# Feed-forward activations turned by VectorE in 32x32 blocks and a trip through a DRAM scratch, in place of TensorE transposes

## The chip, the cores and the metric

The kernel runs on one core of one Trainium2 chip. The metric is the device time of one execution in microseconds (us), lower is better. The kernel before was timed in 3 runs.

## The reference, cut to what matters

The program is a net of four layers on one sequence of 256 rows and 1024 features, in float32. Two layers mix retention, chunked attention and differential attention, two mix an mLSTM with windowed attention. Each layer has one or two gated feed-forward parts, six in all, and only these are touched:

```
ffn = (silu(x @ w_gate) * (x @ w_up)) @ w_down      # x: 256 x 1024
```

The hidden width is 2816 in the two feed-forwards of the first kind of layer, and 2752 in the four of the second kind. TensorE contracts over the partitions of its operands. So the product `silu(...) * (...)`, which comes out with the 256 rows on partitions (two tiles of 128), must stand with its features on partitions before it can be multiplied by `w_down`. Turning it is what the change does in another way.

## The kernel before

**Precision.** All large products are made of float32 values split in two parts: a high part, rounded to the type of TensorE's fast mode, and the rest, the low part. A product takes three matmuls: high by high, high by low, low by high. For weights, ScalarE makes the high part (`wh`, step "hi", line 1270) and VectorE the low part (`wl`, step "lo", line 1499).

**Units.** The weights stream from DRAM in 776 units of mostly 128 x 1024 elements (512 KB), issued by SP (line 1095) into a ring `raw` of 13 slots. The load of unit u+13 waits until TensorE has done unit u. `wh` has 10 slots, so step "hi" of unit u+10 waits for TensorE to be done with unit u. One unit of the feed-forward is two k-tiles of 128 by 512 columns, for two row tiles: 12 matmuls of 512 columns (lines 1957, 1961, 1962).

**The order of work.** A planner writes one list of steps, and each engine walks through the whole list and executes its own part of every step, in that order. `place_splits` puts the "hi" and "lo" steps between the others as far ahead of their unit as the slots allow. Around the end of each large product stand `tail` and `open`: they run the units of a group first for row tile 0 and then for row tile 1, so that the normalization of one tile lies beside the matmuls of the other. In `open` the first 6 to 8 units of a feed-forward go by twice like this.

**One feed-forward** (`plan_ffn`). Its gate and up weights come in 11 chunks of 256 hidden features: four units, which fill two PSUM banks (one for each row tile) with 256 gate and 256 up columns. The pairs of banks alternate. After the units of chunk c the list has:

- `swiglu` (c): ScalarE makes silu into `ffn_s` (line 1465), VectorE multiplies by the up columns into `ffn_a` (line 1887 where the row scale of the norm is applied too, line 1889 otherwise). Both buffers have two slots, by the parity of c.
- `split_act` (c-1): TensorE turns four 128x128 pieces of `ffn_a` by transposes with an identity into a PSUM bank `TB` (line 2018), ScalarE copies it to the high part `act_h` (line 1291), VectorE subtracts to get the low part `act_l` (line 1518; lines 1506 to 1510 for the last chunk of width 192).

The last chunk's `split_act` stands behind the second unit of the down product (`BEHIND = 1`). Then come 22 units of the down product, which read `act_h` and `act_l` as the stationary operand. The transposes that the change takes away are in TensorE's branch

```
elif k == "split_act":
    for r in range(R):
        pe.wait_ge(d_done[2 * st.made.pair + r], st.made.nth + 1)
    src = [b["ffn_a"][:, st.i % 2, r, i * P:(i + 1) * P] for i in range(2) for r in range(R)]
```


Of the kernel before, what the change touches and what calls it, by code (L numbers as in the profile page):

```python
# [32 lines left out]
BEHIND = 1  # L33
# [44 lines left out]
class Step:  # L78

    def __init__(self, kind, after_o=0, after_t=None, apart=None, apply=None, b=None, c=None, dst=None, early=None,  # L80
# [6 lines left out]
        self.kind = kind  # L87
        self.after_o = after_o
# [55 lines left out]
class Plan:  # L144
# [69 lines left out]
    def unit(self, w, lhs, kt0, nk, n, pair, nth, first, last, after_t, form="rows", after_o=0, stacked=None):  # L214
        u = len(self.units)
        self.units.append((w, kt0, nk, n, self.suffix, self.l))
        self.add("unit", u=u, lhs=lhs, kt0=kt0, nk=nk, n=n, pair=pair, nth=nth, first=first, last=last,
                 after_t=after_t, form=form, after_o=after_o, stacked=stacked)
        return u

    def chunk(self, w, lhs, nkt, n, pair, after_t, form="rows", after_o=0):
        nth = self.next_d(pair)
        per = UNIT // n
        groups = [(k, min(per, nkt - k)) for k in range(0, nkt, per)]
        for i, (k0, nk) in enumerate(groups):
            u = self.unit(w, lhs, k0, nk, n, pair, nth, i == 0, i == len(groups) - 1, after_t, form, after_o)
        return Step("chunk", u=u, pair=pair, nth=nth)
# [9 lines left out]
    def pass_first(self, group, upto=None, apart=None):  # L237
# [3 lines left out]
        for st in group:  # L241
            if callable(st):
                st(0)
            elif st.kind == "unit" and (upto is None or i < upto):
                if lead and i == lead[2]:
# [6 lines left out]
                         tiles=(0,), apart=apart)  # L252
# [289 lines left out]
def plan_ffn(p, w_gate, w_up, w_down, width, up_at, t_x, old, new, after_in, chain, turned_of, scaled=None, stats=False,  # L542
# [4 lines left out]
    def turn_chunk(i):  # L547
        turn_of.append(p.next_t())
        p.add("split_act", t=turn_of[i], i=i, width=widths[i], made=chunks[i], n=p.count("hi"))

    kept = p.begin()
    for c in range(nch):
# [5 lines left out]
        chunks.append(p.chunk(sel, "x", KT, 2 * w, p.flip(), t_x))  # L558
        widths.append(w)
        p.add("swiglu", c=chunks[c], i=c, width=w, scaled=scaled, m=p.count("silu", 2) - 2)  # L560
# [15 lines left out]
    for i, (k0, j) in enumerate(order):  # L576
        nk = min(per, kt - k0)
        ends[j] = p.unit((w_down, [(512 * j, 512 * j + 512)]), "act", k0, nk, 512, j, nth[j], k0 == 0,
                         k0 + nk == kt, turn_of[(k0 + nk - 1) // 2], stacked=kt - 1 if width % P else None)
        if i == BEHIND:  # L580
            turn_chunk(nch - 1)
# [294 lines left out]
def build(nc, plan, a):  # L876

    with ExitStack() as ctx:
# [69 lines left out]
        pool_chain = sem("pool_chain")  # L948
        asked = sem("asked")
# [122 lines left out]

        def used(u):
            return plan.units[u][1 + 1] * plan.units[u][3]
# [4 lines left out]
        with nc.Block() as block:  # L1079
            @block.sync  # L1080
            def _(sp):
# [8 lines left out]
                for st in steps:  # L1090
                    if st.kind == "unit":
# [9 lines left out]
                        elif st.u == 7:  # L1101
                            sp.dma_start(b["dmask"][:, :], a["dmask"]).then_inc(dmask_loaded, 16)
                            sp.dma_start(b["b_merge0"][:, :], row("b_merge", 0)[:, 0:D]).then_inc(p_gate[0], 16)
                    elif st.kind == "load":
# [150 lines left out]
            def _(act):  # L1255
# [7 lines left out]
                for st in steps:  # L1263
# [25 lines left out]
                    elif k == "split_act":  # L1289
                        act.wait_ge(t_ready[st.t % 2], st.t // 2 + 1)  # L1290
                        act.activation(b["act_h"][:, 2 * st.i:2 * st.i + 2, :],
                                       TB[st.t % 2][:, :].rearrange("p (k n) -> p k n", k=2), ACT.Copy)\
                           .then_inc(t_hi, 1)
# [175 lines left out]
            def _(dve):  # L1469
# [24 lines left out]
                for st in steps:  # L1494
# [6 lines left out]
                    elif k in ("split", "split_act"):  # L1501
                        dve.wait_ge(t_hi, st.n)
                        bank = TB[st.t % 2][:, :].rearrange("p (k n) -> p k n", k=4 if k == "split" else 2)
                        if k == "split":
                            h, lo = [w[:, st.kg:st.kg + 4, st.tile * P:st.tile * P + P] for w in split_of[st.dst]]
                        elif st.width % P:
                            kt = 2 * st.i
                            dve.tensor_tensor(b["act_l"][:, kt, :], bank[:, 0, :], b["act_h"][:, kt, :].bitcast(F32), ALU.subtract)
                            below = b["act_h"][HALF_P:P, kt + 1, :]
                            dve.tensor_tensor(below, bank[HALF_P:P, 1, :], below.bitcast(F32), ALU.subtract)\  # L1510
                               .then_inc(t_done[st.t % 2], 1)
                            continue
# [362 lines left out]
                    elif k == "swiglu":  # L1875
                        for r in range(R):
# [16 lines left out]
            def _(pe):  # L1893
# [8 lines left out]
                for st in steps:  # L1902
# [4 lines left out]
                    if k in ("unit", "first_tile"):  # L1907
# [63 lines left out]
                    elif k in ("split", "split_act", "turn", "a_turn", "probs_T", "m_log"):  # L1971
# [249 lines left out]
```

## Time and profile before

| | |
|---|---|
| median of 3 runs | 2337.08 us (2336.66 to 2337.7) |
| span of the profiled execution, first to last instruction | 2335.4 us |
| TensorE (PE) busy | 2327.2 us (100%) |
| VectorE (DVE) busy | 1465.5 us (63%) |
| ScalarE (ACT) busy | 1232.3 us (53%) |
| GpSimd (POOL) busy | 127.5 us (5%) |
| granted TensorE clock | 1.000 |
| DMA | 427.47 MB, 183 GB/s mean, 53.8% of 16 engines' span |

The profiled execution has no time of its own beside its span. The three runs lie 1.3 to 2.3 us above the span, their median 1.7 us. Engine names in the rows: PE is the matmul side of TensorE, PEld its weight loads, SPq the issuing of DMAs on SP. Busy matmuls overlap (a matmul of 512 columns shows some 390 ns, and the next starts before it ends), so the distance from one start to the next is what a matmul costs, and the chain of waits shows this distance as its length.

### The profile page before, as it was taken

What the parts mean: (1) busy time and instruction counts of PE and PEld (TensorE: products, weight loads), DVE (VectorE), ACT (ScalarE), POOL (GpSimd) and SP (SyncE); (2) the same over time, 40 slices, a digit from 0 to 9 for tenths busy, and PEclk for the clock granted to TensorE, in tenths of its full rate; (3) what the DMA queues carried; (4) which work ended last, traced back from release to release, by engine and by line L of the source; (5) the groups of instructions that cost most, each with busy time, mean ns of one, the idle gap of its engine ahead of it and who ended that gap; (6) DMA issues with size and microseconds to landing.
All of it is one profiled execution on the core that took longest, in us unless ns stands there. A gap on an engine that the chain in (4) does not pass through costs nothing.

```text
span 2335.4 us, 30302 instructions
## 1 busy us (share of the span) xinstructions
PE 2327.2 (100%) x11568; PEld 1944.3 (83%) x11568; DVE 1465.5 (63%) x2249; ACT 1232.3 (53%) x1910; POOL 127.5 (5%) x141
## 2 busy tenths in 40 slices
PE   9999999999999999999999999999999999999999
PEld 8888888888888888888888888888888888888887
DVE  7556775565567755565487666554755587657554
ACT  6555444445556444354467754544544478555443
POOL 3030000013300000000000000000000000000000
PEclk9999999999999999999999999999999999999999
DMA  8455466555454565565554444655555544445552
GB/s 337 157 194 167 163 210 235 188 181 173 153 206 164 180 222 186 171 218 182 175 184 154 163 153 160 221 182 191 201 182 197 181 163 155 153 171 189 175 195 90
DMA packets 117933, 427.47 MB, mean 183 GB/s; under 512 B 13600, under 2 KB 14240, under 8 KB 116768
## 3 DMA queue, kind: packets, MB, share of 16 engines
q1 hardware_dynamic: 117792, 425.56, 53.8%
q8 instruction: 93, 1.52, 0.3%
q14 instruction: 48, 0.39, 0.1%
HBM read 424.45 MB, written 1.05 MB: 182 GB/s over the span
## 4 chain that ended last, share of the span: by engine, by line
PE 96%; DVE 2%; DMA 1%; ACT 0%; issue 0%; SPq 0%; POOL 0%; DVEq 0%; ACTq 0%
PE bank L1957 27%; PE bank L1962 27%; PE bank L1961 27%; PE bank L2018 4%; PE bank L1944 2%; PE bank L1945 2%; PE bank L1946 2%; DMA raw<-in_weights 1%; DVE wl L1499 1%; PE bank L2107 1%; PE bank L2069 0%; PE bank L2092 0%; PE bank L2040 0%; DVE x L1679 0%; ACT wh L1270 0%; PE bank L2109 0%
## 5 line engine op out<-in xcount | busy, mean ns | idle before, releaser
L1270 ACT ACTIVATE wh<-raw 128x1024 fp32r<-128x1024 f32 (+1 forms) x778 | 816.9, 1053 | 893.4 <-PE bank L1962 826.1
L1499 DVE TENSOR_TENSOR wl<-raw,wh 128x1024 fp32r<-128x1024 f32 (+1 forms) x778 | 937.2, 1224 | 403.3 <-ACT wh L1270 399.7
L1957 PE MATMUL bank<-wh,xh 128*128 128x512 f32 (+1 forms) x2102 | 832.8, 396 | 0.9 <-DVE wl L1499 0.4
L1962 PE MATMUL bank<-wh,xl 128*128 128x512 f32 (+1 forms) x2102 | 817.1, 389 | 0.0
L1961 PE MATMUL bank<-wl,xh 128*128 128x512 f32 (+1 forms) x2102 | 815.4, 388 | 0.0
L1962 PEld LDWEIGHTS bank<-wh,xl 128*128 128x128 f32 x2102 | 394.5, 188 | 82.1
L1957 PEld LDWEIGHTS bank<-wh,xh 128*128 128x128 f32 x2102 | 394.8, 188 | 80.1 <-issue 2.6
L1961 PEld LDWEIGHTS bank<-wl,xh 128*128 128x128 f32 x2102 | 395.3, 188 | 75.3
L1957 PE MATMUL bank<-wh,act_h 128*128 128x512 f32 x528 | 207.1, 392 | 0.0
L1962 PE MATMUL bank<-wh,act_l 128*128 128x512 f32 x512 | 199.4, 390 | 0.0
L1961 PE MATMUL bank<-wl,act_h 128*128 128x512 f32 x512 | 199.2, 389 | 0.0
L1957 PEld LDWEIGHTS bank<-wh,act_h 128*128 128x128 f32 x528 | 99.1, 188 | 20.0
L1962 PEld LDWEIGHTS bank<-wh,act_l 128*128 128x128 f32 x512 | 96.1, 188 | 20.2
L1961 PEld LDWEIGHTS bank<-wl,act_h 128*128 128x128 f32 x512 | 96.2, 188 | 19.4
L1944 PE MATMUL bank<-xh,wh 128*128 128x256 f32 x384 | 110.7, 288 | 0.0
L1946 PE MATMUL bank<-xh,wl 128*128 128x256 f32 x384 | 108.6, 283 | 0.0
L1945 PE MATMUL bank<-xl,wh 128*128 128x256 f32 x384 | 108.6, 283 | 0.0
L1887 DVE SCALAR_TENSOR_TENSOR ffn_a<-bank,scr,ffn_s 128x256 f32<-128x256 f32 (+1 forms) x96 | 39.5, 457 | 74.5 <-ACT ffn_s L1465 74.5
L1944 PEld LDWEIGHTS bank<-xh,wh 128*128 128x128 f32 x384 | 73.5, 191 | 1.4 <-issue 1.0
L1945 PEld LDWEIGHTS bank<-xl,wh 128*128 128x128 f32 x384 | 73.6, 192 | 0.1
L1946 PEld LDWEIGHTS bank<-xh,wl 128*128 128x128 f32 x384 | 73.5, 191 | 0.0
L1204 POOL TENSOR_TENSOR scr<-scr 128x1 f32<-128x1 f32 x12 | 10.2, 852 | 1028.7 <-DVE scr L1677 680.2
(352 smaller groups left out, 2129.8 us busy)
## 6 DMA issues: line engine op xcount, KB each, us to landing
raw<-in_weights SPq DMA_DIRECT2D x760, 512.0 KB, 3.3
raw<-in_weights SPq DMA_DIRECT2D x16, 384.0 KB, 3.1
ln<-in_ln SPq DMA_DIRECT2D x4, 1024.0 KB, 6.1
bias<-in_bias SPq DMA_DIRECT2D x2, 1024.0 KB, 8.5
b_merge<-in_b_merge SPq DMA_DIRECT2D x2, 1024.0 KB, 5.5
gain<-in_gain_ffn SPq DMA_DIRECT2D x4, 512.0 KB, 3.7
decay<-in_decay SPq DMA_DIRECT2D x2, 768.0 KB, 10.3
x<-in_x SPq DMA_DIRECT2D x2, 512.0 KB, 6.3
```

Of the source, the lines that this page charges most:

```text
L1204: pool.tensor_tensor(root[:, r:r + 1], vsum[:, r:r + 1], halves[:, 0:1], ALU.pow).then_inc(rooted, 1)
L1270: act.activation(wh[:, u % NH, 0:used(u)], raw[:, u % NR, 0:used(u)], ACT.Copy).then_inc(hi_done, 1)
L1499: dve.tensor_tensor(wl[:, u % NR, 0:used(u)], raw[:, u % NR, 0:used(u)], wh[:, u % NH, 0:used(u)].bitcast(F32), ALU.subtract).then_inc(lo_ ...
L1887: ins = dve.scalar_tensor_tensor(dst, up, root[:, r:r + 1], s_in, ALU.mult, ALU.mult)
L1944: pe.matmul(out, w_h, lh[:, kt, :], start=st.first and i == 0, stop=False)
L1945: pe.matmul(out, w_h, ll[:, kt, :], start=False, stop=False)
L1946: last = pe.matmul(out, w_l, lh[:, kt, :], start=False, stop=st.last and i == st.nk - 1)
L1957: pe.matmul(out, h, w_h, start=st.first and i == 0, stop=False)
L1961: pe.matmul(out, h, w_l, start=False, stop=False)
L1962: last = pe.matmul(out, lo, w_h, start=False, stop=ends)
L2018: last = pe.transpose(bank[:, i * P:(i + 1) * P], piece, ident[:, :])
L2107: pe.matmul(out, vs[:, 0, :], pt[:, 0:S], start=True, stop=False)
```

## The change

The 32x32 block transpose of VectorE works within 32 partitions. The change splits the turning of a chunk in three:

1. New step `act_block`, right behind `swiglu`: VectorE transposes the 32x32 blocks of `ffn_a`, in two instructions of 128x256 elements (one for each row tile), into `ffn_s`.
2. New step `act_out`: SP waits for VectorE and writes the chunk to a DRAM scratch `turn` in four DMAs, one for each block of 32 partitions (64 KB each, runs of 128 elements, 512 bytes). New step `act_back`: SP waits until all four have landed and reads the chunk back as 128 partitions of 2 KB (256 KB) into `ffn_a`, now with features on partitions.
3. Step `split_act` no longer involves TensorE. ScalarE waits for the read and copies from `ffn_a` (SBUF) instead of from PSUM; VectorE subtracts from the same buffer. TensorE's down units wait for the new semaphore `act_split`.

`act_out` of chunk c-1 stands behind the first unit of chunk c, `act_back` behind the third unit, and `split_act` where it stood, behind `swiglu` (c). For the last chunk they stand behind the first, third and fifth unit of the down product. The order of the units, the slots and all other transposes are as they were.

```diff
-BEHIND = 1
+OUT_AT, BACK_AT, LAST_AT = 0, 2, 4
...
+    def chunk(self, w, lhs, nkt, n, pair, after_t, form="rows", after_o=0, among=None):
+
         nth = self.next_d(pair)
         per = UNIT // n
         groups = [(k, min(per, nkt - k)) for k in range(0, nkt, per)]
         for i, (k0, nk) in enumerate(groups):
             u = self.unit(w, lhs, k0, nk, n, pair, nth, i == 0, i == len(groups) - 1, after_t, form, after_o)
+            if among:
+                among(i)
         return Step("chunk", u=u, pair=pair, nth=nth)
...
     def turn_chunk(i):
-        turn_of.append(p.next_t())
-        p.add("split_act", t=turn_of[i], i=i, width=widths[i], made=chunks[i], n=p.count("hi"))
+        p.add("split_act", i=i, width=widths[i], m=turn_of[i], n=p.count("hi"))
+
+    def moved(i):
+        def among(k):
+            if k == OUT_AT:
+                p.add("act_out", i=i, n=turn_of[i])
+            elif k == BACK_AT:
+                p.add("act_back", i=i, n=turn_of[i])
+        return among
 
...
-        chunks.append(p.chunk(sel, "x", KT, 2 * w, p.flip(), t_x))
+        chunks.append(p.chunk(sel, "x", KT, 2 * w, p.flip(), t_x, among=moved(c - 1) if c else None))
         widths.append(w)
-        p.add("swiglu", c=chunks[c], i=c, width=w, scaled=scaled, m=p.count("silu", 2) - 2)
+        p.add("swiglu", c=chunks[c], i=c, width=w, scaled=scaled, m=p.count("silu", 2) - 2, n=turn_of[c - 2] if c > 1 else None)
+        turn_of.append(p.count("act"))
+        p.add("act_block", made=chunks[c], i=c, n=turn_of[c])
         if c:
             turn_chunk(c - 1)
...
         ends[j] = p.unit((w_down, [(512 * j, 512 * j + 512)]), "act", k0, nk, 512, j, nth[j], k0 == 0,
-                         k0 + nk == kt, turn_of[(k0 + nk - 1) // 2], stacked=kt - 1 if width % P else None)
-        if i == BEHIND:
+                         k0 + nk == kt, None, stacked=kt - 1 if width % P else None, after_a=turn_of[(k0 + nk - 1) // 2])
+        moved(nch - 1)(i)
+        if i == LAST_AT:
             turn_chunk(nch - 1)
...
+
+        def act_in(i):
+
+            return b["ffn_a"][:, i % 2, :, :].rearrange("p r n -> p (r n)").rearrange("p (b m n) -> p m b n", b=4, m=2 * R)
...
+                    elif st.kind == "act_out":
+                        sp.wait_ge(act_turned, st.n)
+                        to = a["turn"][st.i].rearrange("(q j b n) -> b j q n", q=4, j=32, b=4)
+                        for k in range(4):
+                            sp.dma_start(to[k], b["ffn_s"][32 * k:32 * k + 32, st.i % 2, :, :].rearrange("p r n -> p (r n)")
+                                         .rearrange("p (q n) -> p q n", q=4)).then_inc(act_out[st.n % 2], 16)
+                    elif st.kind == "act_back":
+                        sp.wait_ge(act_out[st.n % 2], 64 * ((st.n + 1) // 2))
+                        sp.dma_start(b["ffn_a"][:, st.i % 2, :, :].rearrange("p r n -> p (r n)"),
+                                     a["turn"][st.i].rearrange("(p n) -> p n", p=P))\
+                          .then_inc(act_back[st.n % 2], 16)
...
                     elif k == "split_act":
-                        act.wait_ge(t_ready[st.t % 2], st.t // 2 + 1)
-                        act.activation(b["act_h"][:, 2 * st.i:2 * st.i + 2, :],
-                                       TB[st.t % 2][:, :].rearrange("p (k n) -> p k n", k=2), ACT.Copy)\
-                           .then_inc(t_hi, 1)
+                        act.wait_ge(act_back[st.m % 2], 16 * ((st.m + 1) // 2))
+                        act.activation(b["act_h"][:, 2 * st.i:2 * st.i + 2, :].rearrange("p k (r b n) -> p (k r) b n", r=R, b=4),
+                                       act_in(st.i), ACT.Copy).then_inc(t_hi, 1)
...
-                    elif k in ("split", "split_act"):
+                    elif k == "act_block":
+                        for r in range(R):
+                            dve.wait_ge(d_done[2 * st.made.pair + r], st.made.nth + 1)
+                        to = b["ffn_s"][:, st.i % 2, :, :].rearrange("p r n -> p (r n)").rearrange("p (q k r n) -> p q k r n", q=4, k=2, r=R)
+                        for r in range(R):
+                            last = dve.transpose(to[:, :, :, r, :], b["ffn_a"][:, st.i % 2, r, :]
+                                                 .rearrange("p (k q n) -> p q k n", k=2, q=4))
+                        last.then_inc(act_turned, 1)
+                    elif k == "split_act":
                         dve.wait_ge(t_hi, st.n)
-                        bank = TB[st.t % 2][:, :].rearrange("p (k n) -> p k n", k=4 if k == "split" else 2)
-                        if k == "split":
-                            h, lo = [w[:, st.kg:st.kg + 4, st.tile * P:st.tile * P + P] for w in split_of[st.dst]]
-                        elif st.width % P:
-                            kt = 2 * st.i
-                            dve.tensor_tensor(b["act_l"][:, kt, :], bank[:, 0, :], b["act_h"][:, kt, :].bitcast(F32), ALU.subtract)
-                            below = b["act_h"][HALF_P:P, kt + 1, :]
-                            dve.tensor_tensor(below, bank[HALF_P:P, 1, :], below.bitcast(F32), ALU.subtract)\
-                               .then_inc(t_done[st.t % 2], 1)
-                            continue
+                        h, lo = [w[:, 2 * st.i:2 * st.i + 2, :].rearrange("p k (r b n) -> p (k r) b n", r=R, b=4)
+                                 for w in split_of["act"]]
+                        whole = act_in(st.i)
+                        if st.width % P:
+                            dve.tensor_tensor(lo[:, 0:R], whole[:, 0:R], h[:, 0:R].bitcast(F32), ALU.subtract)
+                            below = h[HALF_P:P, R:2 * R]
+                            dve.tensor_tensor(below, whole[HALF_P:P, R:2 * R], below.bitcast(F32), ALU.subtract)\
+                               .then_inc(act_split, 1)
                         else:
-                            h, lo = [w[:, 2 * st.i:2 * st.i + 2, :] for w in split_of["act"]]
-                        if k == "split" and st.scale != 1.0:
+                            dve.tensor_tensor(lo, whole, h.bitcast(F32), ALU.subtract).then_inc(act_split, 1)
...
                     elif k == "swiglu":
+                        if st.n:
+                            dve.wait_ge(act_split, st.n)
...
+                        if st.after_a:
+                            pe.wait_ge(act_split, st.after_a)
...
-                    elif k in ("split", "split_act", "turn", "a_turn", "probs_T", "m_log"):
+                    elif k in ("split", "turn", "a_turn", "probs_T", "m_log"):
...
-                        elif k == "split_act":
-                            for r in range(R):
-                                pe.wait_ge(d_done[2 * st.made.pair + r], st.made.nth + 1)
-                            src = [b["ffn_a"][:, st.i % 2, r, i * P:(i + 1) * P] for i in range(2) for r in range(R)]
...
+    a["turn"] = nc.dram_tensor("turn", (11, 2 * P * S), F32, kind="Internal").ap()
```

## Rows read from the trace of the kernel before

**Rows 1.** The page: busy time by engine, and the chain that ended last.

```profile
PE 2327.2 (100%) x11568; PEld 1944.3 (83%) x11568; DVE 1465.5 (63%) x2249; ACT 1232.3 (53%) x1910; POOL 127.5 (5%) x141
...
PE 96%; DVE 2%; DMA 1%; ACT 0%; issue 0%; SPq 0%; POOL 0%; DVEq 0%; ACTq 0%
```

**Rows 2.** Waits, whole span: total us, times, longest us.

```profile
ACT wh L1270 <- PE bank L1962: 826.1, 565, 13.9
DVE wl L1499 <- ACT wh L1270: 399.7, 322, 3.2
...
PE bank L2018 <- DVE merged L1703: 0.5, 1, 0.5
PE bank L1957 <- DVE wl L1499: 0.4, 1, 0.4
```

**Rows 3.** Instructions of line 2018 on `ffn_a`: duration ns min/median/max, first and last start.

```profile
L2018 PE MATMUL bank<-ident,ffn_a x264: 270/272/275, 331.2 to 2248.5; 128*128 128x128 f32 x132
```

**Rows 4.** TensorE's timeline around two turns: start us, us.

```profile
331.21 0.60 PE L2018 MATMUL bank<-ident,ffn_a 128*128 128x128 f32 x4
331.57 0.48 PE L1957 MATMUL bank<-wh,xh 128*128 128x512 f32 x1
331.89 0.39 PE L1961 MATMUL bank<-wl,xh 128*128 128x512 f32 x1
...
332.36 0.39 PE L1957 MATMUL bank<-wh,xh 128*128 128x512 f32 x1
...
342.34 0.39 PE L1962 MATMUL bank<-wh,xl 128*128 128x512 f32 x1
342.57 0.60 PE L2018 MATMUL bank<-ident,ffn_a 128*128 128x128 f32 x4
```

**Rows 5.** The chain of waits in the first feed-forward: start us, us.

```profile
342.73 0.44 PE bank L2018 x4
```

**Rows 6.** Windows: us; PE, PEld, DVE, ACT, POOL busy; clock; DMA share; GB/s.

```profile
342.57:353.94 11.37, 11.37 (x53) 9.40 (x52) 6.25 (x7) 5.27 (x7) 0.00 (x0) 1.00 0.56 190
353.94:365.30 11.36, 11.36 (x53) 9.40 (x52) 6.25 (x7) 5.27 (x7) 0.00 (x0) 1.00 0.56 183
...
20.00:40.00 20.00, 20.00 (x90) 16.57 (x89) 13.11 (x12) 13.00 (x16) 4.32 (x5) 1.00 1.03 409
```

**Rows 7.** Groups of instructions: count, busy us, mean ns, idle us before, releaser.

```profile
L1889 DVE TENSOR_TENSOR ffn_a<-ffn_s,bank 128x256 f32<-128x256 f32 x44 | 16.6, 418 | 36.5 <-ACT ffn_s L1465 36.3
L1690 DVE TENSOR_TENSOR merged<-x,gain 128x512 f32<-128x512 f32 x24 | 15.5, 688 | 0.3
L1518 DVE TENSOR_TENSOR act_l<-bank,act_h 128x512 fp32r<-128x512 f32 x62 | 42.9, 692 | 4.1 <-ACT act_h L1291 4.0
L1291 ACT ACTIVATE act_h<-bank 128x512 fp32r<-128x512 f32 x66 | 39.4, 597 | 0.0
L1360 ACT ACTIVATE wide<-x 128x512 f32<-128x512 f32 x32 | 19.9, 626 | 52.7 <-DVE x L1665 40.1 <-DVE x L1663 12.5
```

**Rows 8.** DMAs: the issue of the output on SP (ns), and packets while two outputs were stored (8 us).

```profile
L1183 SPq DMA_DIRECT2D out<-x x4: 332/338/348, 2315.9 to 2333.0; - x4
...
out<-x SPq DMA_DIRECT2D x4, 256.0 KB, 2.0
...
q1 hardware_dynamic: 245, 0.44, 14.4%
```

**Rows 9.** Weight loads (line 1095) on SP in the first down product.

```profile
L1095 SPq DMA_DIRECT2D raw<-in_weights x14: 327/328/328, 402.8 to 439.6; - x14
...
DMA to landing us min/median/max: 3.1/3.3/3.5
```

**Rows 10.** VectorE's, then ScalarE's timeline in the opening of the third feed-forward.

```profile
1003.88 0.88 DVE L1887 SCALAR_TENSOR_TENSOR ffn_a<-bank,scr,ffn_s 128x256 f32<-128x256 f32 x2 [0.49 <-ACT ffn_s L1465]
1004.68 4.85 DVE L1499 TENSOR_TENSOR wl<-raw,wh 128x1024 fp32r<-128x1024 f32 x4
...
1007.20 1.07 ACT L1270 ACTIVATE wh<-raw 128x1024 fp32r<-128x1024 f32 x1 [0.66 <-DMA raw<-in_weights]
...
1011.07 1.06 ACT L1270 ACTIVATE wh<-raw 128x1024 fp32r<-128x1024 f32 x1 [0.33 <-PE bank L1962]
1013.79 1.06 ACT L1270 ACTIVATE wh<-raw 128x1024 fp32r<-128x1024 f32 x1 [1.66 <-PE bank L1962]
```

**Rows 11.** VectorE's timeline in steady chunks of the first feed-forward.

```profile
344.20 0.75 DVE L1889 TENSOR_TENSOR ffn_a<-ffn_s,bank 128x256 f32<-128x256 f32 x2 [1.77 <-ACT ffn_s L1465]
```

More of the change, by code:

```diff
@@ L78, with __init__ @@
 class Step:
-    def __init__(self, kind, after_o=0, after_t=None, apart=None, apply=None, b=None, c=None, dst=None, early=None,
+    def __init__(self, kind, after_a=0, after_o=0, after_t=None, apart=None, apply=None, b=None, c=None, dst=None, early=None,
                  end=None, fed=None, first=None, form=None, g=None, gate=None, h=None, half=None,
@@ L87, in __init__ @@
         self.kind = kind
+        self.after_a = after_a
         self.after_o = after_o
@@ L212, in next_d, with unit @@
         return self.d[pair] - 1
-    def unit(self, w, lhs, kt0, nk, n, pair, nth, first, last, after_t, form="rows", after_o=0, stacked=None):
+    def unit(self, w, lhs, kt0, nk, n, pair, nth, first, last, after_t, form="rows", after_o=0, stacked=None, after_a=0):
         u = len(self.units)
@@ L217, in unit @@
         self.add("unit", u=u, lhs=lhs, kt0=kt0, nk=nk, n=n, pair=pair, nth=nth, first=first, last=last,
-                 after_t=after_t, form=form, after_o=after_o, stacked=stacked)
+                 after_t=after_t, form=form, after_o=after_o, stacked=stacked, after_a=after_a)
         return u
-    def chunk(self, w, lhs, nkt, n, pair, after_t, form="rows", after_o=0):
+    def chunk(self, w, lhs, nkt, n, pair, after_t, form="rows", after_o=0, among=None):
         nth = self.next_d(pair)
@@ L251, in pass_first @@
                          first=st.first, last=st.last, after_t=lead[0] if lead else st.after_t, stacked=st.stacked,
-                         tiles=(0,), apart=apart)
+                         after_a=st.after_a, tiles=(0,), apart=apart)
                 if apart:
@@ L948, in build @@
         pool_chain = sem("pool_chain")
+        act_turned = sem("act_turned")
+        act_out = [sem(f"act_out{i}") for i in range(2)]
+        act_back = [sem(f"act_back{i}") for i in range(2)]
+        act_split = sem("act_split")
         asked = sem("asked")
@@ L1500, in _ @@
                                           wh[:, u % NH, 0:used(u)].bitcast(F32), ALU.subtract).then_inc(lo_done, 1)
-                    elif k in ("split", "split_act"):
-                        dve.wait_ge(t_hi, st.n)
-                        bank = TB[st.t % 2][:, :].rearrange("p (k n) -> p k n", k=4 if k == "split" else 2)
-                        if k == "split":
-                            h, lo = [w[:, st.kg:st.kg + 4, st.tile * P:st.tile * P + P] for w in split_of[st.dst]]
-                        elif st.width % P:
-                            kt = 2 * st.i
-                            dve.tensor_tensor(b["act_l"][:, kt, :], bank[:, 0, :], b["act_h"][:, kt, :].bitcast(F32), ALU.subtract)
-                            below = b["act_h"][HALF_P:P, kt + 1, :]
-                            dve.tensor_tensor(below, bank[HALF_P:P, 1, :], below.bitcast(F32), ALU.subtract)\
-                               .then_inc(t_done[st.t % 2], 1)
-                            continue
-                        else:
-                            h, lo = [w[:, 2 * st.i:2 * st.i + 2, :] for w in split_of["act"]]
-                        if k == "split" and st.scale != 1.0:
+                    elif k == "act_block":
[7 more added lines that the diff above has]
+                    elif k == "split_act":
+                        dve.wait_ge(t_hi, st.n)
+                        h, lo = [w[:, 2 * st.i:2 * st.i + 2, :].rearrange("p k (r b n) -> p (k r) b n", r=R, b=4)
[6 more added lines that the diff above has]
+                               .then_inc(act_split, 1)
+                        else:
+                            dve.tensor_tensor(lo, whole, h.bitcast(F32), ALU.subtract).then_inc(act_split, 1)
+                    elif k == "split":
+                        dve.wait_ge(t_hi, st.n)
+                        bank = TB[st.t % 2][:, :].rearrange("p (k n) -> p k n", k=4)
+                        h, lo = [w[:, st.kg:st.kg + 4, st.tile * P:st.tile * P + P] for w in split_of[st.dst]]
+                        if st.scale != 1.0:
```

## The prediction

> **What bounds the kernel now.** I read the engines' busy times and the chain that ended last first: the reader is to see TensorE busy for 2327.2 of 2335.4 us, and the chain on it for 96% of the span [rows 1]. Then the waits: TensorE waited for VectorE's weight halves once, 0.4 us, while ScalarE waited 826.1 us in 565 places for TensorE to free a slot, and VectorE 399.7 us for ScalarE [rows 2]. So the helpers run as far ahead as their slots let them. An instruction that leaves TensorE's queue gives its time back, and one added elsewhere costs nothing until it has used up that lead.
>
> **What leaves TensorE.** 264 transposes of `ffn_a` [rows 3], in 66 sets of four: 6 feed-forwards of 11 chunks. A set's price is the distance it opens. From one set's start to the next there are 342.57 - 331.21 = 11.36 us, with 4 units of 12 matmuls between [rows 4]. The undisturbed pitch is (342.34 - 332.36) / 44 = 0.2268 us, so the 48 matmuls take 10.89 us, and the set costs 11.36 - 10.89 = 0.47 us. The chain of waits gives 0.44 us for the four [rows 5]; the other 0.03 us is in the matmuls right behind, whose pitch is longer (331.57 to 331.89 is 0.32 us) [rows 4]. The length 270 ns of one transpose [rows 3] overlaps the next and is not its price. 66 x 0.47 = 31.2 us gained; by the chain alone 66 x 0.44 = 29.0 us.
>
> In sentences of their own: the Trainium skill (VectorE: DVE Perf Modes, section Rules for kernel authors) speaks against this change. It says to turn 128x128 on TensorE if a PSUM destination will do, as it did here, and it names VectorE as fastest only for 32x32 within a bank; in the section on the three transpose paths it has 390 ns for TensorE and 311 ns for VectorE, in bf16. By these a set would give back 4 x 390 ns, an estimate of 103 us for the 66 sets. The rows say 0.44 us for four [rows 5], and I go by them.
>
> **What VectorE gets.** Two block transposes of 128x256 for each chunk. The trace has none. From below: 0.42 us, a VectorE instruction of that size (line 1889) [rows 7]. From above: 0.69 us, one of twice that size with all operands in SBUF (line 1690) [rows 7]. I take 0.42, nearest in size, so 0.84 us a chunk (to 1.38), 55 us in all (to 91). VectorE is busy 6.25 us of a chunk [rows 6]; it becomes 7.1 to 7.6 of 10.89. A transpose could take (10.89 - 6.25) / 2 = 2.3 us before VectorE set the pace. The subtraction stays at 0.69 us, since a source in SBUF costs the same (lines 1518 and 1690) [rows 7]. On ScalarE the copy goes from 0.60 to about 0.63 us (lines 1291 and 1360) [rows 7]; it is busy 5.27 us of a chunk [rows 6]. Both are covered by the waits of [rows 2] and cost nothing; without that cover it would be 0.87 us a chunk, 57 us.
>
> **What SP gets.** Five DMAs a chunk, issued in about 0.34 us each [rows 8, 9], beside four weight loads: 9 x 0.34 = 3.1 of 10.89 us. Two waits, and behind both stand the next weight loads. Let T be the end of a chunk's last unit. The multiplication of that chunk ends 344.95 - 342.57 = 2.4 us behind it [rows 4, 11], the block transposes at T + 3.2 to 3.8. `act_out` is reached at T + 2.72 + 0.33 = T + 3.1, so SP waits 0.1 to 0.7 us and has issued four by T + 5.2, just before the next load (T + 5.4). Landing takes 2.0 us for a store alone [rows 8], 3.3 us for a weight load [rows 9]; so the scratch is written by T + 7.2 to 8.5. `act_back` is reached at T + 8.2 + 0.3: no wait, or a short one. The read is back at T + 10.5 to 12, and ScalarE gets to `split_act` only behind the next silu, at about T + 10.9 + 2.0 = T + 12.9. Nothing is late. The weight loads have their own cover: 13 slots against 10 of `wh`, three units or 8.2 us, of which 3.3 are landing; beyond it a late load first eats ScalarE's lead.
>
> **DMA traffic.** The engines are busy 0.56 x 11.36 = 6.4 us of a chunk [rows 6]. Added are 256 KB in 512 packets of 512 bytes and 256 KB in 128 packets of 2 KB. From below, by bytes: 512 KB at the 409 GB/s of the crowded start [rows 6] is 1.3 us. From above: two stores of 256 KB took 14.4% of 8 us = 1.15 us of 16 engines, for 245 packets, that is 0.075 us a packet [rows 8]; 640 such packets on 16 engines are 3.0 us. So 7.7 to 9.4 us of 10.89. I take 3.0, because the packets are small; it hides either way.
>
> A sentence apart: the Trainium skill (DMA: Bandwidth & Descriptors, section Bandwidth) has 0.95 us for a transfer of 64 KB and calls those under that size dominated by descriptors. By it the four writes are an estimate of 3.8 us a chunk, and the DMA engines would be nearly full in the up product. No row here has such a write.
>
> **Openings and ends.** Here the lead is shortest and the weights are tight: in the third feed-forward ScalarE waits up to 0.66 us for a load, while units retire every 1.36 us [rows 10]. But the lead is there. At 1011.07 ScalarE waits for TensorE to free a slot, so it is 10 units ahead [rows 10]; when the first product is done (1004.76) VectorE starts on unit 13 of the feed-forward while TensorE is in unit 4 or 5 of its second pass, about 18 us from needing it (3 x 1.36 + 5 x 2.72). The first chunk's trip comes at the worst place: four writes behind crowded loads land perhaps 5 us after their issue, SP stands still for these, and ScalarE and VectorE wait some 5 us for the read. That is 5 of 18 us. For the last chunk the parts are asked for only by the 21st down unit, 15 units (41 us) behind `split_act`. Cost: zero.
>
> **Sum.** 2335.4 - 31.2 = 2304.2 us of span. The three runs lie 1.3 to 2.3 us above it, so 2306 us; from the median, 2337.1 - 31.2 = 2305.9. By the chain's 0.44 it would be 2308.
>
> **Rivals.**
> 1. *Part of the gain is lost at the openings.* SP's stop for a write, behind loads at full rate, makes a weight load so late that TensorE waits. For it: ScalarE does wait for loads there [rows 10], and SP is one queue. Against: 18 us of cover. If each feed-forward lost 1 to 3 us, the time would be 2312 to 2324 us.
> 2. *The packets decide, and it gets slower.* If a 512 byte packet cost as much as one of 4 KB (6.4 us x 16 / 512 = 0.199 us), the writes would take 6.4 us a chunk and the read 1.6: 14.4 us of DMA against 10.89 of TensorE, 3.5 short. Over 11 chunks that is 38.5 us; the loaded lead of ten units covers 27 us, so TensorE waits 11.5 us in each feed-forward and the time is 2306 + 69 = 2375 us. Slower than before needs 5.2 us of waiting each, an excess of 2.9 us a chunk, a packet price from 0.18 us on. Against: a 2 KB packet costs 0.075 us, less than half [rows 8].
> 3. *VectorE sets the pace.* Block transposes above 2.3 us each, against 0.42 to 0.69. At 4 us each a chunk would take 14.3 us, 3.4 too many; 11 x 3.4 less a lead of some 24 us is 13 us in each feed-forward, so 2386 us. Nothing of 128x256 in the rows comes near.
> 4. *Nothing is gained:* TensorE's pitch lengthens by as much, through more traffic in SBUF (0.47 us over 48 matmuls, 4%). Against: at 409 GB/s the engine issued its matmuls as usual: 90 recorded in 20 us, as dense as at 190 GB/s (53 in 11.37 with four short ones) [rows 6]. The time would be 2337.
>
> **Chances.** Forecast 80%, rival 1 13%, rival 2 4%, rival 3 1%, rival 4 2%. The forecast's own range is 2304 to 2309. With most of rival 1 the range is 2302 to 2322; the low end is a set at 0.5 us and no wait. What a measurement can tell from no change is 0.2%, 4.7 us. Faster by more: 80 + 13 = 93%; within: 2%; slower: 5%.
>
> **What would show it.** Line 2018 on `ffn_a` is gone, and a chunk's period is 10.89 us. TensorE's waits stay at a few us in total. VectorE's busy share rises to about 66%, DMA's by 4 to 7 points. ScalarE's wait for the read is nil in steady chunks and some us at the first chunk of each feed-forward. It would be wrong if TensorE showed waits for `wl` behind late loads, a chunk period over 10.9 us, or block transposes above 2 us.

## The result, and the profile after

| | before | changed |
|---|---|---|
| median | 2337.36 us (2336.66 to 2337.7, 4 runs) | 2306.02 us (2305.03 to 2306.57, 4 runs) |
| profiled execution: time, span | span 2335.4 us | 2305.94 us, span 2304.2 us |
| ratio to before | | 0.9867 (95% interval 0.9853 to 0.988) |

The kernel is 31.3 us faster; 31.2 us and 2306 us were forecast, with a range of 2302 to 2322 us. The page of the changed kernel, the lines that answer to [rows 1] (busy time by engine, the DMA queue, the chain that ended last), with two groups of instructions:

```profile
PE 2295.8 (100%) x11304; PEld 1919.0 (83%) x11304; DVE 1506.7 (65%) x2381; ACT 1234.1 (54%) x1910; POOL 127.7 (6%) x141
...
q1 hardware_dynamic: 165312, 460.18, 59.8%
...
PE 96%; DVE 2%; DMA 1%; ACT 0%; issue 0%; DVEq 0%
...
L2008 PE MATMUL bank<-wh,xl 128*128 128x512 f32 (+1 forms) x2102 | 816.1, 388 | 0.0
...
L1324 ACT ACTIVATE act_h<-ffn_a 128x512 fp32r<-128x512 f32 x66 | 41.6, 630 | 70.6 <-DMA ffn_a<-turn 70.3
```

TensorE has 11568 - 11304 = 264 matmuls fewer, and it is still what the chain runs through for 96%. Its busy time fell by 31.4 us, all of the gain. The big groups are as they were. VectorE is busy for 41.2 us more, at no cost.

TensorE's timeline of the changed kernel shows where the time came from. The first rows here answer to [rows 4]: two starts of the first matmul of a chunk, with 48 matmuls between and nothing else.

```profile
342.22 0.39 PE L2003 MATMUL bank<-wh,xh 128*128 128x512 f32 x1
...
353.10 0.39 PE L2003 MATMUL bank<-wh,xh 128*128 128x512 f32 x1
```

The period is 10.88 us, where it was 11.36 us. The block transposes (duration ns min/median/max) and the changed kernel's DMAs of the trip (count, KB each, median us to landing):

```profile
L1538 DVE STREAM_TRANSPOSE ffn_s<-ffn_a x132: 401/445/447, 329.1 to 2215.4; 128x256 f32<-128x256 f32 x132
```

```profile
turn<-ffn_s SPq DMA_DIRECT2D x264, 64.0 KB, 2.8
ffn_a<-turn SPq DMA_DIRECT2D x66, 256.0 KB, 4.7
```

The waits of the changed kernel (total us, times, longest us) answer to [rows 2]:

```profile
ACT wh L1303 <- PE bank L2008: 716.1, 496, 13.9
DVE wl L1531 <- ACT wh L1303: 289.9, 219, 3.2
...
ACT act_h L1324 <- DMA ffn_a<-turn: 70.3, 50, 3.8
```

ScalarE waits for the read in 50 chunks of 66. That is new, and it was forecast only for the openings. It comes out of time in which ScalarE used to wait for TensorE: that wait fell from 826.1 to 716.1 us. Two timelines of the changed kernel, ScalarE's and then SP's, in a chunk of the third feed-forward, show the trip. The chunk ends at 1009.1, when ScalarE's "hi" step is let go.

```profile
1009.12 1.06 ACT L1303 ACTIVATE wh<-raw 128x1024 fp32r<-128x1024 f32 x1 [0.84 <-PE bank L2008]
1010.08 0.82 ACT L1497 ACTIVATE ffn_s<-bank,scr 128x256 f32<-128x256 f32 x2
...
1022.00 0.63 ACT L1324 ACTIVATE act_h<-ffn_a 128x512 fp32r<-128x512 f32 x1 [0.22 <-DMA ffn_a<-turn]
```

```profile
1012.42 1.84 SPq L1130 DMA_DIRECT2D turn<-ffn_s  x4
1014.49 3.07 SPq L1117 DMA_DIRECT2D raw<-in_weights  x2
1017.61 1.18 SPq L1134 DMA_DIRECT2D ffn_a<-turn  x1
```

Counted from the chunk's end T = 1009.1: the writes are issued from T + 3.3 to T + 5.2 (forecast T + 3.1 to 3.8, and T + 5.2), the read at T + 8.5 (forecast T + 8.5), and the data is there at T + 12.9 (forecast T + 10.5 to 12).

### The profile page after: what moved, and what is told of

Its sections match the earlier page's. It is cut to its first block, busy times and chain, and to the rows that moved or that the text cites. A ratio compares the mean times of both kernels' runs of the same rounds, so it can differ in the third digit from the quotient of the medians.

```text
span 2304.2 us, 30370 instructions
## 1 busy us (share of the span) xinstructions
PE 2295.8 (100%) x11304; PEld 1919.0 (83%) x11304; DVE 1506.7 (65%) x2381; ACT 1234.1 (54%) x1910; POOL 127.7 (6%) x141
## 3 DMA queue, kind: packets, MB, share of 16 engines
q1 hardware_dynamic: 165312, 460.18, 59.8%
## 4 chain that ended last, share of the span: by engine, by line
PE 96%; DVE 2%; DMA 1%; ACT 0%; issue 0%; DVEq 0%
PE bank L2003 28%; PE bank L2008 27%; PE bank L2007 27%; PE bank L2060 3%; PE bank L1990 2%; PE bank L1991 2%; PE bank L1992 2%; DMA raw<-in_weights 1%; DVE wl L1531 1%; PE bank L2149 1%; PE bank L2111 0%; PE bank L2134 0%; PE bank L2082 0%; DVE x L1721 0%; PE bank L2151 0%; ACT wh L1303 0%
## 5 line engine op out<-in xcount | busy, mean ns | idle before, releaser
L1303 ACT ACTIVATE wh<-raw 128x1024 fp32r<-128x1024 f32 (+1 forms) x778 | 814.3, 1052 | 787.4 <-PE bank L2008 716.1
L1324 ACT ACTIVATE act_h<-ffn_a 128x512 fp32r<-128x512 f32 x66 | 41.6, 630 | 70.6 <-DMA ffn_a<-turn 70.3
```

What stands on the lines that cost most here:

```text
L1303: act.activation(wh[:, u % NH, 0:used(u)], raw[:, u % NR, 0:used(u)], ACT.Copy).then_inc(hi_done, 1)
L1324: act.activation(b["act_h"][:, 2 * st.i:2 * st.i + 2, :].rearrange("p k (r b n) -> p (k r) b n", r=R, b=4), act_in(st.i), ACT.Copy).then_i ...
```

## The experiments

The second column of the table is the median, and the third the ratio to the kernel before, timed in the same rounds. "Waits" are those of TensorE for VectorE's writes of `ffn_a`.

| run | us | ratio (95%) | waits, us |
|---|---|---|---|
| changed kernel, again | 2306.4 | 0.9868 (0.9853 to 0.9883) | none |
| e1: and four idle transposes a chunk | 2337.1 | 1.0001 (0.9992 to 1.001) | none |
| e2: before, two transposes a set | 2322.0 | 0.9934 (0.9921 to 0.9946) | none |
| e3: no trip | 2306.2 | 0.9865 (0.9852 to 0.9879) | none |
| e4: read asked for at once | 2305.3 | 0.9863 (0.9847 to 0.988) | none |
| e8: four pairs of block transposes | 2306.5 | 0.9864 (0.9849 to 0.9878) | none |
| e9: six pairs | 2321.7 | 0.9936 (0.9919 to 0.9952) | 10.4 |
| e5: seven pairs | 2378.6 | 1.0176 (1.0161 to 1.0191) | 43.6 |
| e6: nine pairs | 2472.3 | 1.0577 (1.0562 to 1.0593) | 117.0 |
| e7: runs of 128 bytes | 2305.8 | 0.9864 (0.985 to 0.9879) | none |
| e10: runs of 32 bytes | 2426.2 | 1.0371 (1.0355 to 1.0386) | 85.0 |

### Is the gain the transposes' time in TensorE's queue? (e0 to e3)

The changed kernel was run again as a base for the three others.

> The changed kernel as it is, timed beside the three experiments below. Theory A (the 66 sets of transposes leave TensorE's queue at 0.47 us each and the round trip through DRAM is hidden): 2306 us, a ratio of 0.9866 to the kernel before. Theory B (part of the gain is from elsewhere, such as reading the turned chunk from SBUF, or a part is lost to the trip and made up by something else): the same number, so this run only sets the base.

**e1** puts four transposes that nobody reads back into TensorE's queue, by a new step `idle_turn` behind each `split_act`. They go to `SB`, a bank of the attention, so TensorE first checks that its last reader is done.

```diff
+                    elif k == "idle_turn":
+                        pe.wait_ge(s_done, st.s)
+                        for i in range(4):
+                            pe.transpose(SB[:, i * P:(i + 1) * P], ident[:, :], ident[:, :])
```

> The changed kernel, and TensorE also issues four 128x128 float32 transposes of the identity into an unused PSUM bank for each chunk, at the place where the old ones stood; nothing reads them and nothing waits for them. Theory A: all of the gain goes, 2306 + 31 = 2337 us (2335 to 2339). Theory B: some gain stays, as the waits and the PSUM reads of the old way are still gone: 2315 to 2330.

It took 2337.1 us: the whole gain is gone, with block transposes and the trip still in place. TensorE's timeline in e1 shows the old set:

```profile
342.00 0.39 PE L2009 MATMUL bank<-wh,xl 128*128 128x512 f32 x1
342.23 0.60 PE L2021 MATMUL bank<-ident 128*128 128x128 f32 x4
342.59 0.48 PE L2004 MATMUL bank<-wh,xh 128*128 128x512 f32 x1
```

**e2** does half a set in the kernel before.

```diff
-                            src = [b["ffn_a"][:, st.i % 2, r, i * P:(i + 1) * P] for i in range(2) for r in range(R)]
+                            src = [b["ffn_a"][:, st.i % 2, r, i * P:(i + 1) * P] for i in range(1) for r in range(R)]
```

> The kernel before with two transposes in each set instead of four (the second half of every chunk's features is not turned, what is in the bank is used). Theory A with a price by transpose (0.11 us each, the pitch in the chain): half of 29 us, 2337.4 - 14.5 = 2323 us. With a price by set (the change from matmuls to transposes and back costs most): 2330 us or more. In between if 0.03 us of 0.47 belong to the set: 2322 to 2323.

2322.0 us: 15.7 us less than before, half of 31.3. So the price goes by the transpose, 31.3 / 264 = 0.119 us each on average, and little is left for the change from matmul to transpose and back. TensorE's timeline in e2 shows that little:

```profile
331.19 0.38 PE L2018 MATMUL bank<-ident,ffn_a 128*128 128x128 f32 x2
331.32 0.48 PE L1957 MATMUL bank<-wh,xh 128*128 128x512 f32 x1
331.64 0.39 PE L1961 MATMUL bank<-wl,xh 128*128 128x512 f32 x1
...
342.34 0.38 PE L2018 MATMUL bank<-ident,ffn_a 128*128 128x128 f32 x2
```

The period is 342.34 - 331.19 = 11.15 us, 0.21 less than before and 0.27 more than in the changed kernel. The first matmul behind a set of two still takes 331.64 - 331.32 = 0.32 us, as behind a set of four [rows 4]. So some hundredths of a microsecond seem to go by the set and not by the transpose. Over 66 sets that is an estimate of 1 to 3 us, which the run times don't resolve.

**e3** leaves the DRAM trip out.

```diff
-                    elif st.kind == "act_out":
-                    elif st.kind == "act_back":
-            return b["ffn_a"][:, i % 2, :, :]...
+            return b["ffn_s"][:, i % 2, :, :]...
-                        act.wait_ge(act_back[st.m % 2], 16 * ((st.m + 1) // 2))
+                        act.wait_ge(act_turned, st.m)
+                        if st.n:
+                            act.wait_ge(act_split, st.n)
```

The last two lines stand in ScalarE's part of `swiglu`: `ffn_s` is now read until VectorE's subtraction is done. Without the trip the 32x32 blocks stay in their partitions, so the values are not those of the reference; the work of the engines is.

> The changed kernel without the write to DRAM and the read back: ScalarE and VectorE take the chunk from the buffer of the block transposes, with its blocks not exchanged between partitions. Theory A: the trip is hidden, so 2306 us again, within 2 us, though ScalarE's 70 us of waits for the read go. Theory B (the trip takes back a part of the gain): 2295 to 2303 us.

2306.2 against 2306.4 us: the trip, 34.6 MB of it, costs nothing that the runs can tell. Theory B falls with e1 and e3.

### Does SP's standing still cost? (e4)

```diff
-OUT_AT, BACK_AT, LAST_AT = 0, 2, 4
+OUT_AT, BACK_AT, LAST_AT = 0, 0, 4
-            elif k == BACK_AT:
+            if k == BACK_AT:
```

> The changed kernel with the read back asked for directly behind the four writes (behind the first unit of the next chunk instead of the third), so that SP stands still in every chunk until the writes have landed, some 3 us, before it can issue the next weight load. Theory A (three units of cover for weight loads, 8 us, and ten units of lead on ScalarE): 2306 us, and ScalarE's waits for the read fall from 70 us. Theory B (rival 1 of the prediction, SP's stops make weights late): 2310 to 2330 us, with TensorE waiting for `wl`.

2305.3 us. SP waited in every chunk (SP's waits in e4, then two of ScalarE's), and nobody behind it was late enough for TensorE to see it (TensorE waited 0.4 us for `wl` in all):

```profile
SPq L1134 <- DMA turn<-ffn_s: 249.0, 66, 8.6
```

```profile
ACT wh L1303 <- DMA raw<-in_weights: 116.8, 142, 4.8
...
ACT act_h L1324 <- DMA ffn_a<-turn: 37.3, 28, 2.2
```

ScalarE waits less for the read (37.3 for 70.3 us) and more for weights (116.8 for 38.4 us). So rival 1 of the prediction fell: SP could stand still for 249.0 / 66 = 3.8 us in a chunk, and for 8.6 us once.

### How much room has VectorE, and what ends it? (e5, e6, e8, e9)

```diff
-                        for r in range(R):
-                            last = dve.transpose(...)
+                        for again in range(7):        # 9 in e6, 4 in e8, 6 in e9
+                            if again:
+                                link(last)
+                            for r in range(R):
+                                last = dve.transpose(...)
```

> The changed kernel with each chunk's pair of block transposes done seven times over, one pair behind the other with a wait between. By 0.8 to 0.9 us a pair VectorE gets 5 us more in each chunk and needs about 12 to 12.4 us where TensorE needs 10.9; over eleven chunks it falls back by 13 to 17 us. Theory A (the cover is the nine units that the low halves of the weights are ahead, 24 us): nothing is lost, 2306 us. Theory C (the cover is the second pair of PSUM banks: a chunk's multiplication must be done before the chunk after next begins, 10.9 us less the 3 us that it takes anyway, so 8 us): each feed-forward loses 5 to 9 us, 2336 to 2360 us, and TensorE waits for VectorE's writes of `ffn_a`.

> The same with nine pairs: VectorE needs 13.6 to 14.3 us in a chunk and falls back by 30 to 37 us in eleven chunks. Theory A (24 us of cover): 6 to 13 us lost in each feed-forward, 2342 to 2384 us. Theory C (8 us of cover): 22 to 29 us lost in each, 2438 to 2480 us.

2378.6 and 2472.3 us. Theory A is wrong in both. VectorE's timeline in e5, in the first feed-forward, gives the period that it needs, 411.75 - 400.26 = 11.49 us, only 0.6 us over TensorE's (the pairs overlap, seven take 5.61 us), and still 72 us are lost:

```profile
400.26 5.61 DVE L1541 STREAM_TRANSPOSE ffn_s<-ffn_a 128x256 f32<-128x256 f32 x14
405.79 0.65 DVE L1555 TENSOR_TENSOR act_l<-ffn_a,act_h 128x512 fp32r<-128x512 f32 x1
406.36 4.62 DVE L1531 TENSOR_TENSOR wl<-raw,wh 128x1024 fp32r<-128x1024 f32 x4
410.90 0.75 DVE L1936 TENSOR_TENSOR ffn_a<-ffn_s,bank 128x256 f32<-128x256 f32 x2
411.75 5.61 DVE L1541 STREAM_TRANSPOSE ffn_s<-ffn_a 128x256 f32<-128x256 f32 x14
```

TensorE's waits in e5 (us in total, times, longest) name the two lines of the multiplication, and the low halves of the weights hardly at all. So it was the banks that were late, as theory C has it:

```profile
PE bank L2006 <- DVE ffn_a L1934: 29.7, 10, 4.9
PE bank L2006 <- DVE ffn_a L1936: 13.9, 3, 5.8
...
PE bank L2006 <- DVE wl L1531: 0.4, 1, 0.4
```

But 43.6 us of waits are not 72 us. TensorE's timeline in e5 behind one of the two longest waits, and the window around it (PE, PEld, DVE, ACT, POOL busy, granted clock, DMA share, GB/s), show the rest:

```profile
440.06 0.39 PE L2011 MATMUL bank<-wh,act_l 128*128 128x512 f32 x1
...
446.22 0.77 PE L2006 MATMUL bank<-wh,act_h 128*128 128x512 f32 x1 [5.76 <-DVE ffn_a L1936]
...
447.21 0.63 PE L2011 MATMUL bank<-wh,act_l 128*128 128x512 f32 x1
447.63 0.63 PE L2006 MATMUL bank<-wh,act_h 128*128 128x512 f32 x1
...
451.68 0.39 PE L2010 MATMUL bank<-wl,act_h 128*128 128x512 f32 x1
451.91 0.39 PE L2011 MATMUL bank<-wh,act_l 128*128 128x512 f32 x1
```

```profile
446.20:451.00 4.80, 4.78 (x11) 3.79 (x12) 4.61 (x12) 2.52 (x3) 0.00 (x0) 0.50 0.77 300
451.50:460.00 8.50, 8.50 (x39) 7.05 (x38) 6.58 (x8) 3.58 (x4) 0.00 (x0) 1.00 0.71 241
```

After 5.8 us without work TensorE's granted clock is 0.50, the 1.2 GHz level, for 4.8 us: matmuls start 0.42 us apart instead of 0.23. In the whole run TensorE is busy for 2325.9 us against 2295.8, so 30.1 us, and 43.6 + 30.1 = 73.7 is the 74.5 us by which the span grew. For e6 it is 117.0 + 51.3 = 168.3 of 169.1 us, for e9 10.4 + 4.9 = 15.3 of 14.6 us.

The place is telling: 440.1 is the end of the second unit of the down product. The third needs the banks of the last chunk, and only two units (5.4 us) stand between, where chunks have four units (10.9 us) between them. Of the 43.6 us of waits, 29.3 us are at the third down unit, one wait in each of the six feed-forwards.

> The changed kernel with the pair of block transposes done four times over. A pair takes 0.80 us in a row of them (5.61 us for seven pairs in the run with seven), so VectorE needs 11.46 - 3 x 0.80 = 9.1 us where TensorE needs 10.9. Theory C (a chunk's multiplication must be done before TensorE comes back to its banks) and theory A both: 2306 us, no wait of TensorE for `ffn_a`. If instead each microsecond added to VectorE cost something: 6 x 11 x 2.4 us is 158 us, and even a tenth of it would show, 2322 us.

> The same with six pairs: VectorE needs 10.7 us in a chunk, 0.2 us less than TensorE. It does not fall back any more from chunk to chunk, but what it has lost in the opening it doesn't win back. Theory C with the short cover at the end (the third unit of the down product needs the banks of the last chunk, two units or 5.4 us behind it, and the multiplication takes 2.4 us anyway, so 3 us of cover): a wait of 0 to 3 us in each feed-forward, and 1 to 2 us of half clock behind it, 2306 to 2336 us, at one place in each, the third down unit. Theory A: 2306 us.

e8: 2306.5 us, with VectorE busy for 1645.5 us, 139 us more than in the change. e9: 2321.7 us. TensorE's timeline in e9 at the start of the third feed-forward's down product, its first matmul and the first of its third unit:

```profile
1098.01 0.39 PE L2006 MATMUL bank<-wh,act_h 128*128 128x512 f32 x1
...
1106.70 0.47 PE L2006 MATMUL bank<-wh,act_h 128*128 128x512 f32 x1 [3.04 <-DVE ffn_a L1934]
```

The wait begins at 1103.7, two units (5.4 us) behind the first matmul and a little. There were five such waits in six feed-forwards, 10.4 us together, all of them at the third down unit.

The lag behind them comes first from the opening: in the third feed-forward the block transposes of the first two chunks start 6.6 us apart in the changed kernel (995.24 and 1001.81), but 10.2 us apart in e9 (1000.05 and 1010.26), because VectorE can't do more. From there on VectorE needs 10.7 to 10.8 us a chunk and wins back 0.1 to 0.2 us in each. A second part comes at the end of the last four feed-forwards, whose last chunk has 192 features: TensorE is sooner done with it, but the block transposes have their full size. In the third, those of the last two chunks start 8.5 us apart in the changed kernel (1087.78 and 1096.32) and 11.0 us in e9 (1095.65 and 1106.70). The first feed-forward has a spot of this kind in its middle (8.3 against 10.7 us, at its sixth and seventh chunk). The second has neither and has no such wait in e9.

So well below TensorE's pace VectorE's work costs nothing (e8), at 10.7 to 10.8 of 10.9 us the lag stays and shows at the one place with short cover, and above the pace every chunk adds to it.

The half clock does not follow every wait. Of the five in e9, the two longest (3.6 and 3.0 us) had it; behind the others (1.6, 1.6 and 0.6 us) the granted clock stayed at 1.00. Windows of e9, behind the wait of 3.0 us and behind one of 1.6 us:

```profile
1107.70:1109.00 1.30, 1.30 (x4) 1.02 (x4) 1.27 (x4) 0.62 (x2) 0.00 (x0) 0.50 1.00 403
1567.00:1569.00 2.00, 2.00 (x11) 1.64 (x10) 1.93 (x6) 0.79 (x2) 0.00 (x0) 1.00 1.04 414
```

Behind the wait of 3.0 us the matmuls start some 0.25 us apart for 0.8 us (1106.70 to 1107.47), and only then 0.4 us.

Theory C has the mechanism but not the sizes. e5 came out above its range (2336 to 2360 us), since the half clock was not in it, and that e6 lies within its range (2438 to 2480 us) is partly luck, since the pairs were also cheaper than I reckoned.

### When do the writes get too dear? (e7, e10)

```diff
-                        to = a["turn"][st.i].rearrange("(q j b n) -> b j q n", q=4, j=32, b=4)
+                        to = a["turn"][st.i].rearrange("(q m j b n) -> b j (q m) n", q=4, m=4, j=32, b=4)   # m=16 in e10
```

The source side is cut to match (`q=16`, in e10 `q=64`). The scratch then holds a chunk's features in another order, so the values are not those of the reference; the bytes moved are.

> The changed kernel with the four writes cut into runs of 128 bytes instead of 512 (the scratch then holds the features of a chunk in another order): 2048 write packets in a chunk instead of 512. The changed kernel's own price is (59.8% of 2304.2 us less 53.8% of 2335.4 us) / 66 = 1.85 us for 656 packets and 80 that only count the semaphore, 0.040 us a packet. If a short packet costs the same, the writes take 5.1 us, the DMA engines 6.4 + 5.1 + 0.6 = 12.1 of 10.9 us in a chunk: short by 1.2 us a chunk, 13 us in eleven. Theory A (the loads' lead covers 27 us): 2306 us, with DMA near 100% in the up products. Rival 2 of the prediction with a dearer short packet (0.06 us or more: 7.7 us of writes, short by 3.8 us a chunk): 2306 + 6 x (42 - 27) = 2396 us or more.

2305.8 us. The page of e7, its packets and its queue:

```profile
DMA packets 266832, 462.10 MB, mean 201 GB/s; under 512 B 154048, under 2 KB 154688, under 8 KB 265664
...
q1 hardware_dynamic: 266688, 460.18, 62.3%
```

101,376 packets more cost 62.3% of 2303.9 less 59.8% of 2304.2 us, 57 us of 16 engines: 0.009 us for each added packet. So the price of the trip goes mostly with its bytes and not with its packets. (The expectation of e7 counts 656 packets and 80 more for the trip; it has 720 in all, 640 with data.)

The Trainium skill (DMA: Bandwidth & Descriptors, Specifications) gives 512 bytes as the least size for full rate, with a read-modify-write below it. In e7 the runs are a quarter of that, and the DMA engines' time for the trip went from 1.84 to 2.71 us a chunk. That agrees with a lower rate below 512 bytes, but it is far from a cliff; no run here shows what the engines do inside.

> The changed kernel with the four writes cut into runs of 32 bytes: 8192 write packets in a chunk. From runs of 128 bytes (62.3% of 2303.9 us against 59.8% of 2304.2 us, for 101,376 packets more) an added packet costs 0.009 us of an engine; 7680 more are 4.4 us a chunk, and the DMA engines need about 12.3 of 10.9 us. Theory A (the loads' lead of ten units): 2306 us. Theory C: the trip comes back later by 1.4 us in each chunk, ScalarE and behind it VectorE stand at `split_act`, and once they are 3 us late at the last chunk or 8.5 us at another, TensorE waits for `ffn_a`: 8 to 15 us in each feed-forward, 2350 to 2400 us. Rival 2 of the prediction (weights late): the same time, but TensorE's waits are for `wl`.

2426.2 us, slower as theory C had it but above its range (2350 to 2400 us), and the waits are for `ffn_a` (85.0 us), not for `wl` (0.4 us). The reason that I gave was too simple. An added packet cost 0.006 us of an engine and not 0.009, so the DMA engines need less than the 12.3 us a chunk that I reckoned: their share was 64.7% over the run, (64.7% of 2425.2 less 53.8% of 2335.4) / 66 = 4.7 us a chunk, so 11.1 us with the weights. SP's timeline in e10 shows what takes 12.2 us:

```profile
411.00 7.05 SPq L1130 DMA_DIRECT2D turn<-ffn_s  x4
418.09 1.90 SPq L1117 DMA_DIRECT2D raw<-in_weights  x2
421.84 0.33 SPq L1134 DMA_DIRECT2D ffn_a<-turn  x1
422.21 0.91 SPq L1117 DMA_DIRECT2D raw<-in_weights  x2
423.16 4.71 SPq L1130 DMA_DIRECT2D turn<-ffn_s  x2
```

Four issues with 2048 runs each keep SP for 7.05 us (1.8 us in the change), the weight loads and the read take 3.1, and the wait for the landing some 1.9. SP's queue is full, 423.16 - 411.00 = 12.2 us for this chunk, and the trip falls behind.

Why the issues take so long stays open. The number of runs is one reason in question, the other is that the DMA engines are nearly full just then and hold SP back. The issues of line 1130 in e10 (duration ns min/median/max) and the window of the same chunk (DMA share next to last):

```profile
L1130 SPq DMA_DIRECT2D turn<-ffn_s x264: 326/1140/9302, 329.9 to 2347.7; - x132
411.00:423.16 12.16, 9.86 (x44) 7.88 (x43) 6.66 (x9) 4.96 (x7) 0.00 (x0) 1.00 0.90 212
```

All 264 have 2048 runs, and yet one can take 0.33 us or 9.3 us, so the runs alone don't set an issue's time. The DMA share is 0.90 over this chunk, far above the 64.7% of the whole run, and 0.96 to 1.01 from 411 to 416 us, while the writes are issued. No experiment here parts the two.

## Why the prediction was right

- **What bounds the kernel, and the set's price.** TensorE's queue, at 0.47 us a set: 31.2 us forecast (66 x 0.473; with the 0.47 as printed it would be 31.0), 31.3 measured. e1 gives the sum back by putting only the transposes back, e2 halves it. The row's 270 ns is the length of one transpose, and its price is the pitch, 0.12 us. The Trainium skill (VectorE: DVE Perf Modes, The three transpose paths) has 390 ns for one in bf16; the estimate of 103 us worked out from it did not come.
- **VectorE.** Forecast 0.84 us a chunk; the trace has 0.77 us for a pair. Free, as e8 shows even for four pairs.
- **The bound on VectorE was wrong.** The prediction let the two block transposes of a chunk grow to 4.6 us in all before VectorE set the pace, and rival 3 gave VectorE a lead of some 24 us in each feed-forward beyond that. The pace was about right: six pairs take 6 x 0.80 = 4.8 us, and with them VectorE needs 10.7 to 10.8 of 10.9 us. The cover was not, e9 already loses 15 us. The cover is the time until TensorE comes back to a pair of banks, 5.4 us at the down product less the 2.4 us that the multiplication takes anyway. At rival 3's 4 us each the time would have been far above its 2386 us: e6 is at 2472 us with 7.2 us of block transposes in a chunk.
- **SP.** The steps in SP's queue came at the times forecast, to 0.3 us. An issue of a write took 0.43 us (median) instead of 0.34.
- **Landing.** Forecast 2.0 to 3.3 us for both; the writes took 2.8, the read 4.7 us (medians). In e4, where SP issues the read right behind the wait for the writes and no weight load just ahead of it, the read lands in 2.7 us. That fits a read that queues behind that load. Hence ScalarE's 70.3 us of waits for the read, which I had at nil for steady chunks. e3 takes them away and gains nothing.
- **DMA.** Forecast 3.0 us a chunk, between 1.3 and 3.0; measured (59.8% of 2304.2 less 53.8% of 2335.4) / 66 = 1.84 us. Its share rose by 6.0 points, as forecast (4 to 7), though the 3.0 us that was taken would have meant about 9. The Trainium skill (DMA: Bandwidth & Descriptors, Bandwidth) has 0.95 us for 64 KB, which gave the estimate of 3.8 us for the writes alone; the trace has 1.84 us for the writes and the read together.
- **Openings.** Cost forecast zero, and TensorE's waits are some 4 us in all in both traces. ScalarE's longest wait for the read was 3.8 us (forecast 5).
- **Rival 2** (packets decide) fell: the trip's 720 packets took 1.84 x 16 / 720 = 0.041 us each on average, against the 0.199 us that it supposed. **Rival 1** (openings) fell with e4. **Rival 4** (a longer pitch) fell: 10.88 us for 48 matmuls under more traffic.

## What to carry to other kernels

Where one engine is busy for all of the span and the others wait for it, price an edit by the distance that it opens in that engine's queue, not by the length of its instructions, and give the work to whoever has slack, even by way of DRAM. Before relying on the slack, look for what the busy engine asks back first: here it was not the stream of weights, ten units ahead, but a PSUM bank two units later. A wait of the busy engine can cost more than its length: behind waits of 3.0 to 5.8 us (e9, e5) the clock was halved for some microseconds, behind those of 1.6 us and less in e9 it was not.

## What the runs showed of the hardware that I had not expected

- Behind a wait of 5.8 us TensorE's granted clock stood at 0.50 for 4.8 us (e5). Behind waits of 1.6 us it stayed at 1.00 (e9). Over a run the slower matmuls added 30 us to 44 us of waits (e5), 51 to 117 (e6), 36 to 85 (e10).
- Four DMAs of 2048 runs each kept SP for 7.05 us, single ones for 0.33 to 9.3 us (e10). One of 128 runs took 0.43 us (median, the changed kernel).
- An added packet of a DMA write costs little: 0.009 us of an engine for each added by cutting runs from 512 to 128 bytes, and (64.7% of 2425.2 less 59.8% of 2304.2) x 16 / 506,880 = 0.006 us by cutting them to 32 bytes.
- Block transposes of 128x256 in float32 take 0.40 to 0.45 us each and 0.77 us the pair.
